# Attention heads of a two-layer streaming encoder: from one head after another to one stream of query tiles

## The reference, cut to what matters

```python
kv_up = (ckv_all @ p['kv_w_up']).reshape(B, past + L, MLA_HEADS, MLA_NOPE + MLA_V)   # 8 heads, 128 + 128
k_nope, v_all = kv_up[..., :MLA_NOPE], kv_up[..., MLA_NOPE:]
q = rms_norm(hin @ p['mla_w_dq'][j], p['mla_q_norm_g'][j]) @ p['mla_w_uq'][j]        # 384 -> 8 * (128 + 64)
q = q.reshape(B, L, MLA_HEADS, MLA_NOPE + MLA_ROPE)
q_pe = apply_rope(q[..., MLA_NOPE:], cos[:, None], sin[:, None])
...
k_chunk = k_pos // CHUNK                                                             # CHUNK = 64
s = jnp.einsum('bqhn,bkhn->bhqk', qn, k_nope) + jnp.einsum('bqhr,bkr->bhqk', qp, k_pe)
s = s.astype(jnp.float32) * MLA_SCALE
allowed = k_chunk[None, :] <= (qpos // CHUNK)[:, None]
p = jax.nn.softmax(jnp.where(allowed, s, -jnp.inf), axis=-1).astype(v.dtype)
return jnp.einsum('bhqk,bkhv->bqhv', p, v)
```

## Time and profile before

| | us |
|---|---|
| median of 3 runs | 3671.08 (3669.82 to 3676.69) |
| the profiled execution's own time | 3674.14 |
| span of the profiled execution | 3672.3 |

### The profile page before, as it was taken

How to read it: one execution, slowest core, us unless ns; L and a number is a source line. 1 busy time by engine, 2 the same in 40 slices (tenths; PEclk the granted TensorE clock), 3 DMA queues, 4 the chain that set the end, 5 groups by cost and what they waited for, 6 DMA issues and landing times.

```text
span 3672.3 us, 52802 instructions
## 1 busy us (share of the span) xinstructions
PE 3339.1 (91%) x19861; PEld 3026.1 (82%) x19861; DVE 1863.8 (51%) x2614; ACT 1011.0 (28%) x1799; POOL 952.6 (26%) x687
## 2 busy tenths in 40 slices
PE   5999979998897999999986889999985999999996
PEld 2999979997486999999985756665684999999995
DVE  3999956664314555554556532222224455455556
ACT  1222234443204222222224422222213222212223
POOL 0322235552334222222212210000024222222222
PEclk8999989998798999999998987898897999999998
DMA  5444621111210111111111100000020111111111
GB/s 200 162 166 161 236 65 47 36 28 42 93 41 23 45 42 45 46 46 46 40 40 35 44 24 12 12 23 12 12 88 13 51 42 44 46 46 46 43 43 49
DMA packets 83444, 214.22 MB, mean 58 GB/s; under 512 B 9161, under 2 KB 40650, under 8 KB 82194
## 3 DMA queue, kind: packets, MB, share of 16 engines
q1 hardware_dynamic: 32640, 121.79, 10.4%
q10 hardware_dynamic: 50706, 91.07, 7.5%
HBM read 184.12 MB, written 28.71 MB: 58 GB/s over the span
## 4 chain that ended last, share of the span: by engine, by line
PE 77%; DVE 8%; issue 5%; POOL 4%; ACT 4%; DMA 1%; DVEq 0%; ACTq 0%; POOLq 0%; SPq 0%
PE PS L310 18%; PE PS L314 17%; PE PS L313 17%; PE PS L1653 3%; PE PS L1652 3%; PE PS L1678 2%; PE PS L563 2%; PE PS L577 2%; PE PS L1167 2%; DVE CV L2127 2%; DVE CV L2124 2%; POOL TB L478 1%; POOL SUMX L1151 1%; PE PS L1667 1%; ACT X L1188 1%
## 5 line engine op out<-in xcount | busy, mean ns | idle before, releaser
L310 PE MATMUL PS<-HH,WH 128*128 128x354 f32 (+1 forms) x3432 | 1124.4, 328 | 124.1 <-DVE HL L487 64.7
L314 PE MATMUL PS<-HH,WL 128*128 128x354 f32 (+1 forms) x3432 | 1122.0, 327 | 0.0
L313 PE MATMUL PS<-HL,WH 128*128 128x354 f32 (+1 forms) x3432 | 1121.5, 327 | 0.0
L306 POOL TENSOR_TENSOR WL<-RAW,WH 128x1024 fp32r<-128x1024 f32 x197 | 518.8, 2633 | 1385.2 <-ACT WH L301 1384.8
L310 PEld LDWEIGHTS PS<-HH,WH 128*128 128x128 f32 x3432 | 654.4, 191 | 133.1 <-issue 131.2
L313 PEld LDWEIGHTS PS<-HL,WH 128*128 128x128 f32 x3432 | 654.9, 191 | 0.2
L314 PEld LDWEIGHTS PS<-HH,WL 128*128 128x128 f32 x3432 | 652.5, 190 | 0.0
L1440 DVE SCALAR_TENSOR_TENSOR X<-PS,ADA,X 128x354 f32<-128x354 f32 x704 | 330.4, 491 | 438.8 <-PE PS L314 438.7
L310 PE MATMUL PS<-FH,WH 128*128 128x354 f32 (+1 forms) x1056 | 361.5, 342 | 22.6 <-DVE FL L1431 14.4
L301 ACT ACTIVATE WH<-RAW 128x1024 fp32r<-128x1024 f32 x197 | 209.0, 1061 | 593.6 <-PE PS L310 587.8
L313 PE MATMUL PS<-FL,WH 128*128 128x354 f32 (+1 forms) x1056 | 344.3, 326 | 0.0
(11 more groups left out here) (266 smaller groups left out, 4294.6 us busy)
## 6 DMA issues: line engine op xcount, KB each, us to landing
RAW<-ws SPq DMA_DIRECT2D x197, 512.0 KB, 3.5
ADR<-wada ACTq DMA_DIRECT2D x72, 512.0 KB, 4.7
scr<-V ACTq DMA_DIRECT2D x32, 530.0 KB, 3.5
AD<-wada SPq DMA_DIRECT2D x4, 2048.0 KB, 23.5
X<-xT SPq DMA_DIRECT2D x1, 4240.0 KB, 16.9
ZL<-scr ACTq DMA_DIRECT2D x8, 530.0 KB, 3.3
scr<-OH ACTq DMA_DIRECT2D x8, 530.0 KB, 2.8
KF<-scr ACTq DMA_DIRECT2D x8, 512.0 KB, 3.9
```

What stands on the lines that cost most here:

```text
L306: e.tensor_tensor(WL[u][:, :], RAW[:, u, :], WH[u][:, :].bitcast(fp32), ALU.subtract).then_inc(lo_done, 1)
L310: mm = e.matmul(out, WH[w][:, c:c + 128], mh, start=first, stop=False)
L313: e.matmul(out, WH[w][:, c:c + 128], ml, start=False, stop=False)
L314: return e.matmul(out, WL[w][:, c:c + 128], mh, start=False, stop=last)
```

## The change

- **One stream.** The eight heads are written out, without a loop, as one stream of 72 tiles x = 9h + t. `pe_heads` does for each tile: transposes of x, scores of x+2 (of the next head at t = 7 and 8), pieces of the next head's projections, weights times values of x.
- **Pieces.** The next head's key chunks 0 to 3 come at t = 0 to 3, its query chunks at t = 3, 5 and 7, all in PSUM bank 7, one after another, each waiting until the one before is copied. Keys are double (`KT0`, `KT1`); query chunk c overwrites `QT` once the tiles that use it have their scores.
- **Values for four heads.** A slab of its own holds the value weights of four heads: 11 tiles of 128 keys by 512 columns, 6 matmuls each, in `VT` (128 x 11 x 512). Those of heads 0 to 3 are made ahead of the heads, between `rope(2)` and `rope(3)`, in six banks in turn. Those of heads 4 to 7 are made in the stream at head 4, t = 0, in bank 7. There are two slabs more.
- **Mask.** `QPC` becomes `QPX` with 128 rows: rows 0 to 63 hold the head's positional queries, copied by POOL chunk by chunk for every head, rows 64 to 127 an indicator of the first 64 queries of each tile. Rows 64 to 127 of `KPE` hold -1e30 at the last 64 keys of each tile. The positional product then has 128 rows and adds the mask; the one-row product is gone. Both halves come by DMA, issued by ACT.
- The output has one PSUM bank (6) in place of two. POOL splits the low part of head 0's slab after cos(3). Waits have constant counts.

```diff
+    m = np.zeros((64, KEYS + T), np.float32)
+    for t in range(GT):
+        m[t, 128 * t + 64:128 * t + 128] = NEG
+        m[t, KEYS + 128 * t:KEYS + 128 * t + 64] = 1.0
...
+        Q_AT, Q_USED = {3: 0, 5: 1, 7: 2}, (3, 6, 9)
...
+            P_BANK[p_] = n_ % 6 if n_ < len(P_FIRST) else 7
+            P_PREV[p_] = at_bank.get(P_BANK[p_])
...
+        def pe_v(e, B, b):
+            p = ("v", B, b)
+            w, c0 = slab_v(B) % 2, V_TILES[b]
+            if b == 0:
+                all_here(e, (hi_done, slab_v(B) + 1), (lo_done, slab_v(B) + 1))
+            if P_PREV[p]:
+                evacuated(e, P_PREV[p])
+            out = PS[:, P_BANK[p], :]
+            for k in range(LB):
+                c = slice(512 * k, 512 * k + 512)
+                mm = e.matmul(out, CKH[:, k, c0:c0 + 128], WH[w][:, c], start=(k == 0), stop=False)
...
+        def pe_score(e, x):
...
+                e.matmul(out, QT[:, q0:q0 + P], KT[h % 2][:, k0 + s0_:k0 + s0_ + w_], start=True, stop=False)
+                mm = e.matmul(out, QPX[:, q0:q0 + P], KPE[:, k0 + s0_:k0 + s0_ + w_], start=False, stop=True)
...
+        def pe_heads(e):
+            for ch in range(len(KCH)):
+                pe_k(e, 0, ch)
+            for ch in range(NCH):
+                pe_q(e, 0, ch)
+            e.wait_ge(rot_ev, 15)
+            e.wait_ge(c_ld, 64)
+            for p in P_FIRST[-6:]:
+                evacuated(e, p)
+            pe_score(e, 0)
+            pe_score(e, 1)
+            for x in range(NX):
+                h, t = divmod(x, NQ)
+                pe_weights(e, x)
+                if x + 2 < NX:
+                    pe_score(e, x + 2)
+                if (h, t) == (HALF, 0):
+                    for b in range(NV):
+                        pe_v(e, 1, b)
+                if h + 1 < HEADS and t < len(KCH):
+                    pe_k(e, h + 1, t)
+                if h + 1 < HEADS and t in Q_AT:
+                    pe_q(e, h + 1, Q_AT[t])
+                pe_ov(e, x)
...
+                if x + 1 < NX:
+                    vec_normalise(v, x + 1)
                 if t in BIG:
...
+                if x + 2 < NX:
+                    vec_top(v, x + 2)
+                if h + 1 < HEADS and t < len(KCH):
+                    vec_k(v, h + 1, t)
...
             rope(2)
+            all_here(e, (lh_rdy, 4), (ll_rdy, 4), (up_ev, 3 * G_MO))
+            for b in range(NV):
+                pe_v(e, 0, b)
             rope(3)
...
+            a.dma_start(KPE[64:128, :], msk[:, 0:KEYS]).then_inc(c_ld, 16)
+            a.dma_start(QPX[64:128, :], msk[:, KEYS:]).then_inc(c_ld, 16)
...
             pool_cos(p, 2)
             pool_cos(p, 3)
+            split_lo(p, slab_h(0), slab_h(0) % 2)
```

More of the change, by code:

```diff
@@ L1606, in key_blocks @@
             return [(first + m, min(128, nk - 128 * m)) for m in range(-(-nk // 128))]
-        def scores(t):
-            q0, P, k0, nk = QTILES[t]
[L1610 to L1669, removed]
-                if t in BIG:
[L1671 to L1711, removed]
-                ins.then_inc(pt_ev, 1)
-                if t + 2 < NQ:
-                    weights(t + 2)
-                all_here(a, (ov_ps, NQ * h + t + 1))
-                if t == 0:
-                    all_here(a, (o_st[u], 16 * i))
-                a.activation(OH[u][:, q0:q0 + P], PS[:, 6 + t % 2, 0:P], ACT.Copy).then_inc(ov_ev, 1)
-            all_here(a, (ov_ev, NQ * h + NQ))
-            a.dma_start(scr[ds(h, 1), :, :].rearrange("a p n -> p (a n)"), OH[u][:, :]).then_inc(o_st[u], 16)
@@ new lines, in pe_k @@
+        def pe_k(e, h, ch):
+            p = ("k", h, ch)
+            n, (c0, cw) = slab_h(h), KCH[ch]
+            if ch == 0:
+                all_here(e, (hi_done, n + 1), (lo_done, n + 1))
+            if P_PREV[p]:
+                evacuated(e, P_PREV[p])
+            for k in range(LB):
+                mm = three(e, PS[:, P_BANK[p], 0:cw], n % 2, 128 * (QB + k), CKH[:, k, c0:c0 + cw], CKL[:, k, c0:c0 + cw], k == 0, k == LB - 1,
+                           ch == 0 and k == 0)
+            mm.then_inc(pj_ps, 1)
@@ new lines, in pe_ov @@
+        def pe_ov(e, x):
+            h, t = divmod(x, NQ)
+            P = QTILES[t][1]
+            evacuated(e, ("v", h // HALF, NV - 1))
+            e.wait_ge(pt_ev, x + 1)
+            past(e, pu_ev, nbig(x + 1))
+            past(e, ov_ev, x)
+            blocks = key_blocks(t)
+            c = 128 * (h % HALF)
+            for m, (b, kw) in enumerate(blocks):
+                mm = e.matmul(PS[:, 6, 0:P], VT[0:kw, b, c:c + 128], PT[0:kw, m, 0:P], start=(m == 0), stop=(m == len(blocks) - 1))
+            mm.then_inc(ov_ps, 1)
@@ new lines, in act_pt @@
+        def act_pt(a, x):
+            t = x % NQ
+            P = QTILES[t][1]
+            a.wait_ge(pt_ps, x + 1)
+            past(a, ov_ps, x)
+            full = [m for m, (b, kw) in enumerate(key_blocks(t)) if kw == 128 and m < 4]
+            rest = [(m, kw) for m, (b, kw) in enumerate(key_blocks(t)) if kw < 128]
+            ins = a.activation(PT[:, 0:len(full), 0:P], bank(4, 128, P)[:, 0:len(full), :], ACT.Copy)
+            for m, kw in rest:
+                ins = a.activation(PT[0:kw, m, 0:P], PS[0:kw, 4, m * 128:m * 128 + P], ACT.Copy)
+            ins.then_inc(pt_ev, 1)
@@ L1906, in pool_rest @@
                 ins = p.memset(OH[u][:, SEQ:SAM], 0.0)
-            with p.Fori(0, HEADS // 2) as i:
-                for u in range(2):
-                    pool_head(p, i, u)
+            pool_heads(p)
             pool_split_run(p, S_MO + 1, KB)
```

248 lines of the change are left out of this document (188 added, 60 removed).

## The result

The changed kernel takes 3495.86 us (median of 4 runs, 3492.75 to 3500.77) against 3673.89 us for the kernel before (4 runs, 3669.82 to 3678.17): a ratio of 0.9517, 95% interval 0.9499 to 0.9534. The profiled execution of the changed kernel took 3497.4 us where that of before took 3674.1: 176.7 us less. I had said 130 less, 3544, and no less than 3518. The direction was right, the size was not, and the range missed it by 22 us.

What follows compares the result with a forecast made beforehand. PE was taken to bound the heads, through work, gaps and a clock averaging 0.86. From the profiled 3674.1 us the terms summed to -130.3, giving 3544 us; the range was 3518 to 3598.

Steps and rivals of the forecast that it cites:

- values: Value projection in the heads: two blocks of 66 512-column matmuls replace 66 128-column ones a head, one block ahead; -43.3 us.
- one-row mask products: Score tiles in the heads: 64 one-row mask matmuls go, each holding PE 0.42 us; -26.9 us.
- rows of the positional product: Score matmuls in the heads: giving the positional product 128 rows instead of 64 costs nothing; 0 us.
- clock: Heads' stage: 149 us at low clock lose 68.6; 8 us kept for start and stray falls; -61, bounds 0 and -69.
- gaps: PE idle time in the heads: 30.3 us go, 21.5 come back from new waits and bank 7; net -8.8 us.
- start: Head 0's projection begins later, at 2139.5 instead of 2129.8, behind value block 0, rope(3) and POOL; +9.7, or +17 at low clock.
- over 1.05 us: Sign of being wrong: score matmuls with 128 rows in the heads take over 1.05 us.
- The clock falls as often as before: Rival for the heads: short gaps keep the low-clock share at 0.28, giving 3593 us; chance 0.22.
- Hand-overs as the bound: Rival for the heads: tile chains or bank 7 end last at every piece, 46 us more, 3590; chance 0.08.
- the low clock that stays: Rival for the heads: bank 7 gaps hold 1.2 GHz, slower than before from share 0.58, up to 3863 us; chance 0.03.
- the value block that does not fit: Rival ahead of the heads: value block 0 begins only after rope(3), in the open, giving 3552 us; chance 0.07.
- 49 us apart: Sign of being right: starts of heads 2 to 4 lie some 49 us apart.

## Why the prediction was wrong, point by point

| term | forecast, us | measured, us | from |
|---|---|---|---|
| values | -43.3 | -43 | wide matmuls 0.233 apart |
| one-row mask products | -26.9 | about -27 | 67 of 68 for mask and row changes together, undone in the stream |
| rows of the positional product | 0 | -40 | 64 rows again: 41.8, 37.3 |
| clock | -61 | about -65 | mean 0.99 for 0.86 |
| gaps | -8.8 | -14 | 19.1 of idle time (without the 5.0 at the start) for 33.0 |
| start | +9.7 | +9.9 | head 0's first key matmul at 2139.69 |
| sum | -130.3 | -179 | 175.3 in the stage, 176.7 in all |

The measured terms add up to 4 us more than the stage lost. The clock's term comes from means of two digits, which alone leave it open by some 2 us either way, and the one for the rows by as much.

**The step that failed** is "That the positional product gets 128 rows for 64 costs nothing where both kinds are seen". I compared the price of a 64-row product with that of its 128-row neighbour, found both at 1.05 us, and concluded that rows are free. Both were dear for the same reason, that they stood side by side. What the runs showed in its place: a product beside one with another number of rows takes 1.05 us, beside one with the same number 0.86, and so the step was worth 40 us and not nothing. The clue was in the trace of before: 512 columns took 1.05, and 256 columns of tile 5, at the same clock, 0.63.

```profile
2241.57 0.70 PE L1653 MATMUL PS<-KPE,QPC 64*128 64x256 f32 x2
2242.20 0.48 PE L1656 MATMUL PS<-MSK 1*128 1x128 f32 x2
```

Half the columns were not half the time, so each product had a fixed part of some 0.2 us, and PEld, which I did not open for these lines, showed both loads of a product starting only with it. I even bounded the cost on the dear side ("Were rows to cost", and a sign of being wrong only for "over 1.05 us") and not on the other. A gain of up to 0.2 x 208 below nothing would have moved the lower end of the range from 3518 to 3476, with the measured 3496 inside.

**Values**: right. The line through two widths gave 0.233; the trace has it, here in the second block, whose tiles are also the 2.35 us apart that 1.40 and 0.95 make:

```profile
2313.62 0.39 PE L1670 MATMUL PS<-WL,CKH 128*128 128x512 f32 x1
2313.85 0.40 PE L1671 MATMUL PS<-WH,CKL 128*128 128x512 f32 x1
2314.94 0.50 PE L1667 MATMUL PS<-WH,CKH 128*128 128x512 f32 x1 [0.69 <-ACT VT L1770]
...
2317.29 0.50 PE L1667 MATMUL PS<-WH,CKH 128*128 128x512 f32 x1 [0.69 <-ACT VT L1770]
```

The 0.216 of the Trainium skill (TensorE: Matmul & The Clock Gate, Back-to-back issue gap), set beside mine there, is that section's figure for matmuls without weight loads of their own between them, and would have been one microsecond a block off. The 131 ns that it gives for a stream of loads and 512-column matmuls does not fit 0.233 here.

**Clock**: the size was right but for 4 of the 8 us I kept back, the reason only in part, so some of the agreement is luck. I named what stood before each fall: narrow value matmuls, gaps, sparse first tiles with one-row products. With the value matmuls thinned out the clock fell as before (0.83), and with the gaps kept and 128-row products it held (0.98). What counted of the three were the sparse tiles, their one-row products and, unnamed, their 64-row ones. That the stream would hold the clock better was right too: without the mask part it has 0.96. That the mask part alone would do the same I did not see. Widening the value matmuls saved no clock against the kernel before, where each 7 us of them ran at 1.00; but left narrow in blocks for four heads they would have run at the low level for the most part.

**Gaps**: right in kind. The new waits came to 19.1 where 21.5 was forecast; the query chunks waited 0.9 each, not 1.1. Of the old ones I left out those ahead of a head's projections, 2.6 us that went too (in total, times, longest):

```profile
PE PS L310 <- ACT OH L1718: 2.6, 7, 0.4
```

**Start**: right. The +17 that I gave for a first block at the low clock was too little by my own 46%: 15.4 us of work would then take 28.5, 13 more, so +23. The block ran at 1.00. POOL's order cost what it was priced at:

```profile
2134.87 2.42 POOL L1585 TENSOR_TENSOR QPE<-QPE,COSN 128x1060 f32<-128x1060 f32 x1 [15.02 <-PE PS L1565]
2137.24 2.34 POOL L309 TENSOR_TENSOR WL<-RAW,WH 128x1024 fp32r<-128x1024 f32 x1
...
2139.69 0.63 PE L313 MATMUL PS<-CKH,WH 128*128 128x354 f32 x1 [4.96 <-issue]
```

**The rivals.** "The clock falls as often as before" had 0.22, and for it the rule of the Trainium skill (TensorE: Matmul & The Clock Gate, A second HAM failure mode: psum-queue depth-cycling). It did not happen, and this trace does not agree with the rule: in the second value block, ten gaps of 0.7 us in a row, the clock stayed at its high level. PE alone, changed kernel:

```profile
2312.00:2340.00 28.00, 20.35 (x79) 1.00 0.10 38
```

Hand-overs as the bound, the low clock that stays, and the value block that does not fit did not happen either. Among the signs I listed, "49 us apart" for the head starts was a slip: my own terms make 44; they are 40 apart, and the difference is again the row changes.

**The range** reached only to where a term came out worse than taken; apart from the clock and the waits nothing in it could come out better. The values, the one-row products and the start, which I could price from rows, held within 1 us each, the clock and the gaps came out 4 and 5 us better, and the price that I set to nothing was off by 40.

**What stays open.** Why rows count for the clock, and how the few falls in the small tiles come about with one 64-row product at a time, was not settled. Fewer rows also change the numbers that the softmax and the matmuls behind it work on, and no run holds these fixed. In the old loop the mask part gave 113 us where 46% of the low time it saved and the 67 us of work make some 125. Of the 12, 3 are idle time of PE in the stage (35.1 us for 32.2) and 4 lie outside the stage, which became 116.7 us shorter; for the rest I have no cause.

## What to carry to other kernels

Before pricing a matmul from its row, fit a line through two widths: a fixed part of 0.2 us a product was a neighbour with another number of rows, and padding a 64-row operand to 128 (here with the mask, which also saved a matmul of its own) removed it. An edit that "costs nothing" needs a bound below nothing too, taken from the engine's other half, the weight loads. And look at the granted clock beside the busy time, and ask which matmuls in that stretch use few rows or few columns.

## What the runs showed of the hardware

- A change between 128-row and 64-row matmuls kept the next weight load from running ahead: at the high clock 1.05 us a float32 product of 512 columns instead of 0.86. Between products of equal rows, 64 or 128, it is 0.86.
- TensorE's clock depended on the rows that the score matmuls use: with the same columns and order its mean over the stage was 0.92 with both products over 64 rows (0.90 when repeated), 0.82 over 32, and 1.00 over 128. With one of the two over 64 rows it was 0.99.
- 128-column matmuls with a new weight load each ran at 1.00 for 7 us a head. In a block of some 60 us they ran at 1.00 for 6.4 us and then at 0.50, 0.21 us each instead of 0.11; a block that began at 0.50 stayed there, with PE recorded as busy throughout.
- In the 512-column value block, with PE idle 0.7 of every 2.35 us, the clock stayed at 1.00.
